# The long convolution as one transform of 2048 odd frequencies: eight phases on PE, combined on DVE by a radix-8 step

## The reference, cut to what matters

```python
def _bidir_long_conv(u, h_past, h_future, skip):
    L = u.shape[1]
    k = jnp.concatenate([h_past, jnp.zeros_like(h_past[:1]), h_future[:0:-1]], axis=0)
    U = jnp.fft.rfft(u32, n=2 * L, axis=1)
    K = jnp.fft.rfft(k, axis=0)
    y = jnp.fft.irfft(U * K[None], n=2 * L, axis=1)[:, :L]
    return (y + u32 * skip).astype(u.dtype)

def _hyena_mixer(z, short_w, short_b, skip, ...):
    v, x1, x2 = jnp.split(_short_conv(z, short_w, short_b), 3, axis=-1)
    filt = _hyena_filters(...)      # sines of an MLP over positions, times a decay
    y = x1 * _bidir_long_conv(v, filt[:, 0, 0], filt[:, 1, 0], skip[0])
    return x2 * _bidir_long_conv(y, filt[:, 0, 1], filt[:, 1, 1], skip[1])
```

## Time and profile before

| | |
|---|---|
| median of 3 runs | 2890.5 us (2888.61 to 2894.37) |
| the profiled execution | 2889.84 us, of it the span 2888.0 us |
| PE busy in the span | 2721.6 us (94%) |
| DVE, ACT busy | 2270.1 us (79%), 1534.1 us (53%) |
| mean granted clock of TensorE | 0.972 |

### The profile page before, as it was taken

One profiled execution on the slowest core, in us unless ns is written; L12 is line 12 of the kernel. 1 busy time (PEld: TensorE's weight loads), 2 busy tenths in 40 slices (PEclk: granted clock), 3 DMA queues, 4 the chain that ended last, 5 costly groups with the idle time before them and its releaser, 6 DMA issues.

```text
span 2888.0 us, 34673 instructions
## 1 busy us (share of the span) xinstructions
PE 2721.6 (94%) x13665; PEld 2227.2 (77%) x13665; DVE 2270.1 (79%) x2113; ACT 1534.1 (53%) x1446; POOL 130.9 (5%) x147
## 2 busy tenths in 40 slices
PE   7999979989999989983999999999999999999997
PEld 2877878856677778772888888888888888888885
DVE  4674189917889865648888888898888889888887
ACT  4432056622222111223777777777777777777774
POOL 0011000000000100000000000000000000000000
PEclk9999999999999989986999999999999999999998
DMA  7498733144546766326999999999999999999994
GB/s 268 158 323 299 224 70 74 44 145 137 188 158 199 290 240 226 111 104 263 373 391 376 367 384 390 380 366 378 389 382 371 366 395 389 374 365 386 391 374 181
DMA packets 205661, 815.03 MB, mean 282 GB/s; under 512 B 32127, under 2 KB 93927, under 8 KB 127104
## 3 DMA queue, kind: packets, MB, share of 16 engines
q1 hardware_dynamic: 185652, 693.25, 64.4%
q0 software_dynamic: 19696, 119.56, 12.2%
q10 hardware_dynamic: 158, 0.07, 0.0%
HBM read 745.43 MB, written 67.39 MB: 281 GB/s over the span
## 4 chain that ended last, share of the span: by engine, by line
PE 50%; ACT 2%; issue 1%; DVE 1%; DVEq 0%; ACTq 0%
PE moe_ps_gate L2025 17%; PE moe_ps_up L2025 15%; PE moe_ps_y L2015 15%; PE moe_ps_h L1996 1%; ACT moe_w_hi L2066 1%; PE moe_ps_x L1988 0%; DVE raw L2188 0%; ACT moe_xt_hi L2059 0%; DVE moe_w_lo L2118 0%; DVE moe_h L2139 0%; ACT moe_sl L2079 0%; PE moe_ps_up L2049 0%; PE moe_ps_gate L2051 0%; PE moe_ps_gate L2049 0%; PE moe_ps_up L2051 0%
## 5 line engine op out<-in xcount | busy, mean ns | idle before, releaser
L2118 DVE TENSOR_TENSOR moe_w_lo<-raw,moe_w_hi 128x2048 fp32r<-128x2048 f32 x528 | 1207.7, 2291 | 159.6 <-ACT moe_w_hi L2066 159.0
L2066 ACT ACTIVATE moe_w_hi<-raw 128x2048 fp32r<-128x2048 f32 x528 | 1011.1, 1920 | 379.3 <-PE moe_ps_gate L2025 127.9
L2025 PE MATMUL moe_ps_up<-moe_w_hi,moe_xt_hi 128*128 128x512 f32 (+1 forms) x768 | 292.5, 381 | 0.0
L2025 PE MATMUL moe_ps_gate<-moe_w_hi,moe_xt_hi 128*128 128x512 f32 (+1 forms) x768 | 289.4, 377 | 1.4 <-DVE moe_xt_lo L2109 1.4
L2025 PE MATMUL moe_ps_gate<-moe_w_hi,moe_xt_lo 128*128 128x512 f32 (+1 forms) x768 | 286.8, 373 | 0.0
L2025 PE MATMUL moe_ps_up<-moe_w_hi,moe_xt_lo 128*128 128x512 f32 (+1 forms) x768 | 286.6, 373 | 0.0
L2025 PE MATMUL moe_ps_gate<-moe_w_lo,moe_xt_hi 128*128 128x512 f32 (+1 forms) x768 | 286.3, 373 | 0.0
L2025 PE MATMUL moe_ps_up<-moe_w_lo,moe_xt_hi 128*128 128x512 f32 (+1 forms) x768 | 286.1, 373 | 0.0
L2015 PE MATMUL moe_ps_y<-moe_w_hi,moe_ht_hi 128*128 128x512 f32 x704 | 218.7, 392 | 0.0
L2015 PE MATMUL moe_ps_y<-moe_w_lo,moe_ht_hi 128*128 128x512 f32 x704 | 217.2, 390 | 0.0
L2015 PE MATMUL moe_ps_y<-moe_w_hi,moe_ht_lo 128*128 128x512 f32 x704 | 217.1, 390 | 0.0
(11 more groups left out here) (284 smaller groups left out, 4366.0 us busy)
## 6 DMA issues: line engine op xcount, KB each, us to landing
raw<-in_w_moe SPq DMA_DIRECT2D x528, 1024.0 KB, 7.3
hyena_g_parts<-gw_d POOLq DMA_DIRECT2D x48, 1024.0 KB, 5.7
proj_w_mod<-in_w_mod SPq DMA_DIRECT2D x32, 512.0 KB, 7.4
gw_d<-proj_g_parts POOLq DMA_DIRECT2D x16, 1024.0 KB, 7.5
hyena_g_late<-gw_d POOLq DMA_DIRECT2D x16, 1024.0 KB, 9.1
w_in<-in_w_in SPq DMA_DIRECT2D x12, 1024.0 KB, 8.1
norm_w_mod<-in_w_mod SPq DMA_DIRECT2D x16, 512.0 KB, 5.8
proj_g_raw<-in_w_in SPq DMA_DIRECT2D x16, 512.0 KB, 10.1
```

The source lines that it names most:

```text
L2025: mm = pe.matmul(ps, hp[:, e % 2, k, :], wp[:, r, :], start=(k == 0 and x == 0), stop=(k == KD - 1 and x == 2))
L2066: act.activation(w_hi[:, g % PARTS], raw[:, g % RAW], ACT.Copy).then_inc(hi_ready, 1)
L2118: dve.tensor_tensor(w_lo[:, g % PARTS], raw[:, g % RAW], w_hi[:, g % PARTS].bitcast(F32), ALU.subtract).then_inc(lo_ready, 1)
```

## The change

The transform is no longer block by block. The 1024 tokens are stored by phase: phase r (of `PH` = 8) holds tokens r, r+8, r+16, ..., 128 of them. One transform of length `FFT` = 2048 at 1024 odd frequencies is made of eight leaves: PE transforms each phase to 128 frequencies (real and imaginary), and DVE combines the eight by `transform`, a radix-8 step over tiles `spec[n]` of [128, 8, 2, 256]. The same step serves filter, input and (after the product, at phase (8-r)%8) the output, so it runs three times for each pass. The product is then one complex multiplication without a sum over blocks. Windows, `win`, `uf`, `t1`, `t2` are gone.

The order is written anew too: for each pass PE goes through eight segments of the next filter, then the four inverses of the running pass, then turns and inputs of the passes in `U_AT`; gate units are placed by `SHARE`. The units now use 4 weight slots all the time, and `h_parts` arrives in four pieces. Decay (1 MB for a half of the channels) and gate (1 MB) are loaded once for each pass. The constants are `dft` [128, 8, 3, 128] (1.5 MB) and `idft` [128, 8, 2, 128] (1 MB). `convolve` writes its last step by phase, with a scratch tile `taken`, and `merge` reads `y_t` by phase and writes it in order.

```diff
@@ norm_and_project: convolve
                     dve.wait_ge(evacuated, bank(u, c, 1) + 1)
+                    if ch:
+                        dve.wait_ge(conv_ready, ch)
+                    dt.then_wait(dve.tensor_scalar(taken[:], z_pad[:, c, 1:T + 1], w(1),
+                                                   par[:, C_SB + ch:C_SB + ch + 1], ALU.mult, ALU.add))
+                    dt.then_wait(dve.scalar_tensor_tensor(out=taken[:], in0=z_pad[:, c, 0:T], scalar=w(0),
+                                                          in1=taken[:], op0=ALU.mult, op1=ALU.add))
                     if u:
                         dve.wait_ge(stored[c], 16 * u)
...
+                    dve.scalar_tensor_tensor(out=conv[:, c].rearrange("p (r m) -> p m r", r=PH),
+                                             in0=z_pad[:, c, 2:T + 2].rearrange("p (m r) -> p m r", r=PH), scalar=w(2),
+                                             in1=taken[:].rearrange("p (m r) -> p m r", r=PH), op0=ALU.mult, op1=ALU.add
+                                             ).then_inc(conv_ready, 1)
@@ hyena: the share of gate units (segments, inverses, inputs, end)
+        U_AT = {-1: (0, 1), 0: (2,), 1: (3,), 2: (), 3: ()}
+        SHARE = {
+            -1: ((0, 0, 0, 0, 0, 0, 0, 0), (0, 0, 0, 0), ((0, 0, 0, 0), (1, 1, 1, 1)), 2),
+            0: ((1, 0, 1, 0, 1, 0, 1, 0), (1, 0, 5, 0), ((1, 0, 1, 0),), 4),
+            1: ((1, 0, 1, 0, 1, 0, 1, 0), (1, 0, 5, 0), ((1, 0, 1, 0),), 3),
+            2: ((1, 0, 1, 0, 1, 0, 1, 0), (1, 0, 5, 0), (), 6),
+            3: ((1, 1, 1, 1, 1, 2, 2, 2), (0, 0, 0, 0), (), 0),
+        }
@@ hyena: POOL
+                def load_h(x):
+                    if x:
+                        pool.wait_ge(g_done, N_BLOCKS * x)
+                    for s in range(KD // 2):
+                        k = slice(2 * s, 2 * s + 2)
+                        pool.dma_start(h_parts[:, :, k], a["hq_d"][x][:, :, k]).then_inc(h_in[s], 16)
+
                 for n in range(N_G):
+                    if n >= G_SLOTS:
+                        pool.wait_ge(g_done, n - G_SLOTS + 1)
+                    if n % N_BLOCKS == G_SLOTS - 1 and n >= N_BLOCKS:
+                        load_h(n // N_BLOCKS)
+                    pool.dma_start(g_parts[:, n % G_SLOTS], a["gw_d"][n % N_BLOCKS]).then_inc(g_in[n % G_SLOTS], 16)
+                    if n == 0:
+                        load_h(0)
@@ hyena: PE
+                def segment(q, r):
+                    x = PH * q + r
+                    past, future = (0, 1) if r <= PH // 2 else (1, 0)
+                    pe.wait_ge(tap_used, x + 1)
+                    to = bank(("seg", q, r))
+                    back = (PH - r) % PH
+                    for pl in range(2):
+                        pe.matmul(to[:, pl], dft[:, r, pl, :], seg[:, x % SEGS, past], start=True, stop=False)
+                        mm = pe.matmul(to[:, pl], dft[:, back, 2 * pl, :], seg[:, x % SEGS, future], start=False, stop=True)
+                    mm.then_inc(a_done, 1)
+                def inputs(q, i):
+                    pe.wait_ge(a_used, a_at["turn", q, i] + 1)
+                    for r in (2 * i, 2 * i + 1):
+                        to = bank(("input", q, r))
+                        for pl in range(2):
+                            mm = pe.matmul(to[:, pl], dft[:, r, pl, :], u_tok[:, r % 4], start=True, stop=True)
+                        mm.then_inc(a_done, 1)
+                def outputs(p, i):
+                    n = NB * p + i
+                    pe.wait_ge(y_ready, p + 1)
+                    if n >= 2:
+                        pe.wait_ge(out_used, n - 1)
+                    for c in range(2):
+                        for s in range(2):
+                            r = 2 * i + s
+                            for pl in range(2):
+                                mm = pe.matmul(ps_out[:, n % 2, c * BLK + s * P:c * BLK + (s + 1) * P],
+                                               spec[Y_SPEC[p]][:, (PH - r) % PH, pl, c * P:(c + 1) * P],
+                                               idft[:, r, pl, :], start=(pl == 0), stop=(pl == 1))
+                    mm.then_inc(out_done, 1)
@@ hyena: DVE (sum_of is one tensor_tensor; aside makes the next decayed segment)
+                def transform(src, mid, aside):
+                    sum_of(z[:, 0:4], x[:, 0:4], x[:, 4:8])
+                    sum_of(z[:, 4:8], x[:, 0:4], x[:, 4:8], ALU.subtract)
+                    aside()
+                    dt.wait()
+                    sum_of(x[:, 4:6], z[:, 0:2], z[:, 2:4])
+                    sum_of(x[:, 6:8], z[:, 0:2], z[:, 2:4], ALU.subtract)
...
+                    for slots, by in ((slice(1, 8, 6), ROOT_HALF), (slice(5, 2, -2), -ROOT_HALF)):
+                        dt.inc(dve.scalar_tensor_tensor(out=z[:, slots], in0=turned[:], scalar=by, in1=x[:, 0:3:2],
+                                                        op0=ALU.mult, op1=ALU.add))
+                    aside()
+                    dt.wait()
+                def products(p, aside):
+                    k, u, z = spec[K_SPEC[p]], spec[U_SPEC[p]], spec[Y_SPEC[p]]
+                    for half in (slice(0, 4), slice(4, 8)):
+                        re, im = (k[:, half, x].unsqueeze(2).broadcast_to([P, 4, 2, HALF_C]) for x in range(2))
+                        dt.inc(dve.tensor_tensor(z[:, half], im, u[:, half], ALU.mult))
+                        dt.wait()
+                        dt.inc(dve.tensor_tensor(u[:, half], re, u[:, half], ALU.mult))
+                        aside()
+                    dt.wait()
+                    dt.inc(dve.tensor_tensor(u[:, :, 0], u[:, :, 0], z[:, :, 1], ALU.subtract))
+                    dt.inc(dve.tensor_tensor(u[:, :, 1], u[:, :, 1], z[:, :, 0], ALU.add))
+                    aside()
+                    dt.wait()
...
+                for p in range(PASSES):
+                    products(p, decay_next)
+                    transform(U_SPEC[p], Y_SPEC[p], decay_next)
+                    dve.sem_inc(y_ready, 1)
+                    for r in coming:
+                        decayed(q, r)
+                    if q < PASSES:
+                        dve.wait_ge(a_used, a_at["seg", q, PH - 1] + 1)
+                        transform(K_LEAF[q], K_SPEC[q], nothing)
                     for i in range(NB):
+                        gated(p, i)
                     if q < PASSES:
+                        dve.wait_ge(a_used, a_at["input", q, PH - 1] + 1)
+                        transform(U_LEAF[q], U_SPEC[q], nothing)
@@ merge
+        def in_order(b, out, src, *more):
+            if b:
+                return out, src, *more
+            by_token = "p (m r) -> p m r"
+            return (out.rearrange(by_token, r=PH), src.rearrange("p (r m) -> p m r", r=PH),
+                    *(x.rearrange(by_token, r=PH) for x in more))
```

More of the change, by code:

```diff
@@ L1062, in hyena @@
         h2, w3, dft, idft, consts_in = (keep[n] for n in ("h2", "w3", "dft", "idft", "hyena_in"))
[L1063 to L1072, removed]
-        u_tok = m.sb("u_tok", [P, 4, HALF_C])
[L1074 to L1078, removed]
+        decay = m.sb("decay", [P, PH, HALF_C])
+        SEGS = 2
+        seg = m.sb("seg", [P, SEGS, 2, HALF_C])
+        spec = [m.sb(f"spec{n}", [P, PH, 2, HALF_C]) for n in range(5)]
+        turned = m.sb("turned", [P, 2, 2, HALF_C])
+        u_tok = m.sb("u_tok", [P, 4, HALF_C])
+        gate = m.sb("gate", [P, 2, T])
+        G_SLOTS = 4
+        g_parts = m.sb("g_parts", [P, G_SLOTS, 2, KD, P], F32R)
         h_parts = m.sb("h_parts", [P, 2, KD, QUARTER], F32R)
@@ L1091, in hyena @@
             sems(n) for n in ("a_done", "a_used", "tap_done", "tap_used", "out_done", "out_used", "yf_ready"))
-        decay_in, gate_in, LOADED = keep["w_mod_in"][0:2], keep["w_mod_in"][2:4], 16 * MOD_CHUNKS
-        a_order = []
[L1096 to L1100, removed]
-                a_order += [("input", q, i // 2, pl) for pl in (i % 2 * 2, i % 2 * 2 + 1)]
@@ new lines, in hyena @@
+        assert next(counter) == N_G
+        a_order = []
+        for p in range(-1, PASSES):
+            if p + 1 < PASSES:
+                a_order += [("seg", p + 1, r) for r in range(PH)]
+            for q in U_AT[p]:
+                a_order += [("turn", q, 0)]
+                for i in range(NB):
+                    if i + 1 < NB:
+                        a_order += [("turn", q, i + 1)]
+                    a_order += [("input", q, 2 * i), ("input", q, 2 * i + 1)]
+        a_at = {what: n for n, what in enumerate(a_order)}
@@ L1273, in _ @@
+                    for r in range(PH):
+                        for n in AT_SEG[p, r]:
+                            gates(n)
+                        if p + 1 < PASSES:
+                            segment(p + 1, r)
+                            x = PH * (p + 1) + r + 2
+                            if x < PH * PASSES:
+                                taps(x)
+                    for i in range(NB):
+                        for n in AT_OUT[p, i]:
```

(13 more changed lines are left out.)

412 lines of the change are left out of this document (183 added, 229 removed).

## The result

The changed kernel takes 2787.65 us (median of 4 runs, 2785.88 to 2791.64), the kernel before beside it 2892.27: a ratio of 0.9642, 95% interval 0.9625 to 0.9658. The forecast was 2788. The profiled execution took 2786.69 us, its span 2784.6.

The account below looks back on a forecast made before the run. PE was taken to bound the stage: 331 us of work plus 48.5 of waits is 379.5 for 484.2 (-104.7); merge +2 gives -102.7, so 2788 us. Forecast's own range 2768 to 2806; whole range 2766 to 2818.

Parts of the forecast that it names:

- PE's work left: Long convolution stage: PE's work falls by 108.0 us through cheaper segments, inputs and inverses, leaving 331 us.
- lowered clock: Long convolution stage, after PE's wait at its start: 6 us lost to lowered clock; none would be 0.
- bank stalls of turns and inputs: Turns and inputs alternate over two PSUM banks, each freed after ACT's copy: 6 us of PE waits, bounds 0 and 12.
- `h_parts`: PE waits for the next quarter's load at units 16, 32 and 48: 11 us together, bounds 3 and 20.
- stores and gate load: Last run of 17 gate units: `g_out` stores 4 us, gate load ahead of them 4; together 8, bounds 0 and 15.
- PE bounds and its cut pays in full: Long convolution stage: PE sets the pace, so its 108.0 us less work counts, less new waits; chance 0.72.
- DVE's step and product: DVE in the stage: a radix-8 step 15.2 us, a product 13.6, 282 us in all, under PE's 331.
- The rivals of 1.2 and 1.7 times the price: DVE's steps and products cost more: 1.2 times, +18 to +25 us (chance 0.09); 1.7 times, 2897, slower than before (0.03).
- PE stays the bound by 1 to 4 us a pass: Passes of the stage: DVE's chain fits under PE's work with 1 to 4 us to spare; pass 0's segments come out even.
- PE over 95% busy from the second pass on: Sign in the profile after that the forecast is right: PE over 95% busy in the stage from the second pass.
- Queues: Rival: stores and loads pace all runs of gate units, 3.45 us each instead of 2.91; +20 us, 2808; chance 0.12.
- The strided reads: Merge reading `y_t` with a step of 128 numbers: +2 us, bounds 0 and 4.6; rival of costlier strided edits: 0.03.

Follow-up runs that it names:

- experiment 1: The changed kernel with every segment's four matmuls issued twice: 2846.46 us.
- Experiments 4 and 5: Two runs of the kernel before: first with half of PE's transform work left out, 2830.88 us; then with half of DVE's product sum left out, 2874.95 us.
- Experiment 2: The changed kernel with three more DVE operations (3.75 us) ahead of each of the 12 radix-8 steps: 2806.91 us.
- second profile: Profile from running the changed kernel again, unchanged, as yardstick for later variants: median 2788.02 us, ratio 0.9641 to the kernel before.
- late units: The changed kernel with the gate units between turns and inputs of passes 0 and 1 placed late instead of alternately: 2776.13 us, ratio 0.9601 to the kernel before.
- experiment 6: The changed kernel with the merge reading and writing `y_t` in stored order, in contiguous runs: 2784.38 us, ratio 0.9639 to the kernel before.
- experiment 7: The changed kernel with `convolve`'s last step writing in token order instead of by phase: 2783.59 us, ratio 0.9645 to the kernel before.

## Why the prediction was right, point by point

| term | forecast | measured |
|---|---|---|
| PE's work left | 331 | prices confirmed: 0.22, 0.109 a record; +59 for the segments doubled |
| start (first segment near 601) | 12.5 | 9.9: first segment at 598.15, less 0.85 for its taps |
| lowered clock | 6, at the start alone | 5 at the start (72 us at 0.93); 5.3 behind the holes at units 16 and 32, and 2 behind unit 48 (192 records take 25.5 us where 0.121 each would be 23.2) |
| bank stalls of turns and inputs | 6 | 1.5 |
| `h_parts` | 11 (2.5, 2.5, 6) | 15.1 (4.1, 4.5, 6.6) |
| stores and gate load | 8 | 5.7 |
| handshakes, last inverses | 5 | 1.0: 0.4 for segments, and 7.54 for 64 records where 7.0 was counted |
| **stage** | **379.5 (-104.7)** | **377.8 (-106.4)** |
| merge | +2 | +3.7 |
| elsewhere | 0 | -0.7 |
| span | -102.7 | -103.4 |

- *PE bounds and its cut pays in full:* right for the cut itself (experiment 1). Experiments 4 and 5 speak for it that DVE's cut was needed as well; the forecast's own sum of DVE's chain had that in it.
- *DVE's step and product:* one step takes 636.34 - 621.26 = 15.1 us, forecast 15.2. The rivals of 1.2 and 1.7 times the price did not come. Experiment 2 tries the first of them: 45 us on 237 of steps and products are 1.19 times, and cost 19 us where the rival had +18 to +25. Its total was right and its place wrong: 13.2 of it come in the first stretch, and each loop gives 1 to 2 (up to 4 by the second profile) where the rival had put 5 to 8.
- *"PE stays the bound by 1 to 4 us a pass":* PE is the bound there, but the size was low. In the changed kernel the slack is 8 to 16 us, because the holes lend it; once they are gone, 4 and 1 are left by the estimate above. The first stretch has none, as "even" had said; added work of either engine comes through there entirely.
- *"PE over 95% busy from the second pass on":* this sign missed. The windows give 95, 95, 91 and 87% (87.18 of 92, 83.26 of 88, 68.44 of 75, 44.47 of 51). Without the holes of the first two loops (late units) the first two windows have 99% each.
- *Queues:* the stretches move 232 to 267 GB/s, as the rival said (232), and gate units between them still run at PE's pace: 120 records in 14.48 us are five units of 2.90. The rival fell; only the last run of 17 units waits for its stores.
- *Sizes that missed:* the bank stalls (a quarter of the estimate) and `h_parts` (15.1 for 11). The lowered clock behind holes was no term of the sum at all; it was paid for by the terms that came smaller. The second profile has 12.6 for `h_parts` and 8.2 for the stores, so single terms differ by 2.5 us from one execution to the next. That the total came out within 2 us while parts missed by up to 6 is in part luck: the total is better than its parts. With 331 the measured terms, without the 2 us behind unit 48, add up to 374.5; of the 3.3 us to 377.8 those 2 are most, and the rest is gaps too small for the list of waits.
- *The strided reads:* 3.7 us, within the bounds of 0 and 4.6 and above the 2 that I took; experiment 6 gives exactly the 3.7 back. `convolve`'s is hidden (experiment 7). The rule of lines on the Trainium skill's page "SBUF — State Buffer", section "Door 1: The DMA port swizzle", had given 4.6 by half rate, an estimate; the trace agrees in kind, but shows 1.6 times on DVE (1927 for 1220 ns) and 1.86 on ACT (1942 for 1044), not 2 on either.

What stays open: how much of the last stretch's spread belongs to the stores, to the gate load in front of them, or to when `h_parts` lands. No run took the gate load out of SP's queue alone. A third slot for `g_out` was not tried.

## What to carry to other kernels

Cut the engine that bounds and the one behind it together: here either alone gave 62 or 15 us, and the whole change, with both and a new order, 105. After such a change, look for work that still waits for a reused buffer, because the shortened stage has less in between; moving other work of the same engine in front of that wait cost nothing and gave 12 us. Look for slack stretch by stretch: where two engines are even, added work of either comes through, though both have idle time on average. And price a hole on PE at its length plus the lower clock behind it: here 3.1 to 4.5 us of waiting cost 4.8 to 7.2.

## What the runs showed of the hardware

- A step of 128 numbers (512 bytes) between neighbouring elements costs 1.6 times on DVE, whether it is read (1927 ns for 1220) or written (2083 for 1285), and 1.86 times on ACT (1942 for 1044), for fp32 tiles of 128x1024. Reversed slots (1221 ns for 1024 elements) and broadcasts (2262 and 2292 ns for 2048), both with inner runs of 256 numbers, cost what plain operands cost (1220 and 2287).
- Two holes of 2.31 and 1.76 us with 6 records between them were enough to bring the granted clock to its lower level for the records behind (0.53 from 722 to 726 us), from 1.00 before (710 to 718). In the second profile one hole of 2.77 us did the same (0.50 in the 2.2 us behind it, 1.00 again from 726).
- An inverse of 128-column fp32 records with new weights each time runs at 0.109 us a record, half of a 256-column one (0.216): its price went with the columns, so loading weights did not set it.
